# Projection slabs as one 512-column product with the high weights and one of 256 with the low: a bank per quarter of the outputs

## The reference

```python
IN_SPLITS = (GROUP_W, GROUP_W,                              # RG-LRU: gate, input
             GROUP_W, GROUP_W, GROUP_W,                     # short gated convolution: b, c, h
             GLA_HEADS * GLA_DK, GLA_HEADS * GLA_DK, GROUP_W, GROUP_W, GLA_RANK,   # GLA: q, k, v, g, rank 16
             GROUP_W, GROUP_W, GROUP_W)                     # attention: q, k, v
o = o * lax.rsqrt(jnp.mean(o * o, -1, keepdims=True) + RMS_EPS)      # end of GLA
...
return o * jax.nn.silu(g)
...
for e in range(N_EXPERTS):
    h = jax.nn.silu(xt @ w_gate[e]) * (xt @ w_up[e])
    out = out + combine[:, e:e + 1] * (h @ w_down[e])
```

## Time and profile before

| | |
|---|---|
| median of 3 runs | 1715.86 us (1712.81 to 1719.31) |
| profiled execution | 1714.94 us, its span 1713.2 us |
| PE busy | 1553.8 us, 91% of the span |
| DVE busy | 945.7 us, 55% |
| ACT busy | 546.2 us, 32% |
| projections | to about 387 us, and again from about 858 to 1229 us |
| granted TensorE clock, mean | 0.962 of 2.4 GHz |

### The profile page before, as it was taken

How to read it: one execution, slowest core, us unless ns; L and a number is a source line. 1 busy time by engine, 2 the same in 40 slices (tenths; PEclk the granted TensorE clock), 3 DMA queues, 4 the chain that set the end, 5 groups by cost and what they waited for, 6 DMA issues and landing times.

```text
span 1713.2 us, 38421 instructions
## 1 busy us (share of the span) xinstructions
PE 1553.8 (91%) x16224; PEld 1090.1 (64%) x16224; DVE 945.7 (55%) x1548; ACT 546.2 (32%) x694; POOL 50.2 (3%) x36
## 2 busy tenths in 40 slices
PE   8999999998899999966599999999997999996664
PEld 8999999884444555422299999998743555452221
DVE  7657655647455556623466476566374556652235
ACT  4553543323222222201265544533321222221112
POOL 0004000000000000000000050000000000000000
PEclk9999999999999999988899999999999999998887
DMA  8655556659999999999965555567589999999996
GB/s 296 216 169 191 170 177 223 244 212 383 420 420 421 420 420 421 420 421 420 396 201 185 165 194 178 162 240 294 235 347 420 420 421 421 421 420 420 421 421 250
DMA packets 138709, 543.88 MB, mean 317 GB/s; under 512 B 23012, under 2 KB 26312, under 8 KB 88536
## 3 DMA queue, kind: packets, MB, share of 16 engines
q1 hardware_dynamic: 138196, 541.97, 81.0%
q10 hardware_dynamic: 388, 0.04, 0.0%
HBM read 539.88 MB, written 2.10 MB: 316 GB/s over the span
## 4 chain that ended last, share of the span: by engine, by line
PE 68%; SPq 15%; DMA 10%; DVE 4%; issue 1%; DVEq 1%; ACT 1%; ACTq 0%
PE ps L826 23%; PE ps L1102 11%; PE ps L988 10%; SPq L408 10%; PE ps L1120 6%; PE ps L823 5%; DMA room<-in_w_up_dram 5%; DMA room<-in_w_down_dram 4%; SPq L412 4%; PE ps L1044 3%; PE ps L1059 3%; PE ps L1079 1%; PE ps L1052 1%; DVE room L1160 1%; DVE w_lo L1160 1%
## 5 line engine op out<-in xcount | busy, mean ns | idle before, releaser
L1102 PE MATMUL ps<-room 128*32 128x256 f32 x5344 | 336.4, 408 | 91.9 <-DMA room<-in_w_up_dram 91.5
L1160 DVE TENSOR_TENSOR w_lo<-room,w_hi 128x2048 fp32r<-128x2048 f32 (+1 forms) x121 | 276.2, 2292 | 228.9 <-ACT w_hi L535 228.4
L1102 PEld LDWEIGHTS ps<-room 128*32 128x32 f32 x5344 | 193.0, 116 | 244.6 <-DMA room<-in_w_up_dram 87.6
L826 PE MATMUL ps<-hT_hi,w_hi 128*128 128x256 f32 x1152 | 329.7, 286 | 1.1 <-DVE w_lo L1160 0.7
L826 PE MATMUL ps<-hT_lo,w_hi 128*128 128x256 f32 x1152 | 326.0, 283 | 0.0
L826 PE MATMUL ps<-hT_hi,w_lo 128*128 128x256 f32 x1152 | 325.9, 283 | 0.0
L535 ACT ACTIVATE w_hi<-room 128x2048 fp32r<-128x2048 f32 x120 | 228.0, 1911 | 228.4 <-PE ps L826 101.7
L1160 DVE TENSOR_TENSOR h<-h,ps 128x512 f32<-128x512 f32 (+1 forms) x380 | 241.7, 698 | 13.7 <-PE ps L1059 13.6
L1160 DVE TENSOR_TENSOR room<-room,ps 128x128 f32<-128x128 f32 (+2 forms) x53 | 18.5, 353 | 400.1 <-ACT room L742 396.7
L826 PEld LDWEIGHTS ps<-hT_hi,w_hi 128*128 128x128 f32 x1152 | 220.9, 192 | 4.7 <-issue 2.4
L826 PEld LDWEIGHTS ps<-hT_hi,w_lo 128*128 128x128 f32 x1152 | 221.0, 192 | 0.7 <-issue 0.5
(11 more groups left out here) (254 smaller groups left out, 1650.0 us busy)
## 6 DMA issues: line engine op xcount, KB each, us to landing
room<-in_w_down_dram SPq DMA_DIRECT2D x116, 1024.0 KB, 22.0
room<-in_w_gate_dram SPq DMA_DIRECT2D x114, 1024.0 KB, 25.3
room<-in_w_up_dram SPq DMA_DIRECT2D x114, 1024.0 KB, 26.8
room<-in_w_in_dram SPq DMA_DIRECT2D x88, 1024.0 KB, 5.0
room<-in_w_out_dram SPq DMA_DIRECT2D x32, 1024.0 KB, 5.2
spare<-in_w_gate_dram SPq DMA_DIRECT2D x14, 1024.0 KB, 24.8
spare<-in_w_up_dram SPq DMA_DIRECT2D x14, 1024.0 KB, 26.7
spare<-in_w_down_dram SPq DMA_DIRECT2D x12, 1024.0 KB, 17.9
```

What stands on the lines that cost most here:

```text
L826: last = eng.matmul(ps[:, b + o // 2, (o % 2) * T:(o % 2) * T + T], w_[:, o * P:o * P + P], x_[:, kk, :], start=opens and o % 2 == 0, stop ...
L1102: last = eng.matmul(ps[r0:r0 + BLK, 0, 0:2 * P], xe[:, x0:x0 + BLK], unit_gu(u)[:, :, k, c * P:c * P + P], start=(i == 0 and k == 0), stop ...
L1160: return eng.tensor_tensor(o, a, b, op)
```

## The change

Seven slabs (`MERGED`: 1, 3, 4, 5, 7, 8, 9) use w_hi once for both halves of the input. hT_hi and hT_lo become one buffer, `hT_parts`, and the product of the high weights has 512 moving columns, 256 of the high and 256 of the low input, which land side by side in a bank. The low weights then add to its first 256 columns. Each of the four outputs so has a bank of its own (0 to 3), and the sum of its two halves is made later: ACT copies the cross half (`copy_cross`), DVE adds the first half to it (`add_cross`) and counts `bank_free`. Silu and Gelu are then applied in place. Slabs 0, 2, 6 and 10 keep their form and all use banks 0 and 1. At its first quarter a slab waits bank by bank; slabs 1, 3 and 7 begin with outputs 2 and 3.

```diff
+    MERGED = (1, 3, 4, 5, 7, 8, 9)
+    EVACUATED = (0, 2, 5, 6, 7)
...
+                def copy_cross(s, dst, scale=1.0):
+                    for o in range(4):
+                        if o < 3:
+                            eng.wait_ge(o_done.sem, o_done.at(l, 3 * MERGED.index(s) + o + 1))
+                        else:
+                            eng.wait_ge(w_used.sem, w_used.at(l, 4 * s + 4))
+                        eng.activation(dst[:, o * T:o * T + T], ps[:, o, T:2 * T], ACT.Copy, scale=scale
+                                       ).then_inc(cross_copied.sem, 1)
+
+                def in_place(s, dst, func):
+                    eng.wait_ge(bank_free.sem, freed(l, s))
+                    for i in range(2):
+                        eng.activation(dst[:, i * 512:i * 512 + 512], dst[:, i * 512:i * 512 + 512], func
+                                       ).then_inc(z_evac.sem, 1)
...
+                copy_cross(1, r_x)
                 rounds(11, 12)
-                evacuate(1, r_x)
...
-                rounds(18, 20)
+                rounds(18, 19)
                 eng.wait_ge(qk_ready.sem, qk_ready.at(l, 1))
-                evacuate(3, a_qT, scale=float(P) ** -0.5)
+                copy_cross(3, a_qT, scale=float(P) ** -0.5)
+                rounds(19, 20)
...
-                rounds(25, 28)
-                evacuate(5, c_g, ACT.Silu)
+                rounds(25, 27)
+                copy_cross(5, c_g)
+                rounds(27, 28)
+                in_place(5, c_g, ACT.Silu)
...
-                rounds(34, 36)
-                evacuate(7, r_g, ACT.Gelu_apprx_tanh)
+                rounds(34, 35)
+                copy_cross(7, r_g)
+                rounds(35, 36)
+                in_place(7, r_g, ACT.Gelu_apprx_tanh)
...
-                    if first == 0 and s >= 2:
-                        eng.wait_ge(z_evac.sem, z_evac.at(l, 2 * (s - 2) + 2))
...
+                        order = (2, 3, 0, 1) if q == 0 and s in (1, 3, 7) else range(2 if token_major else 4)
+                        for ks, o in itertools.product(parts, order):
...
+                            if q == 0 and s:
+                                bank = o if token_major or joined else o // 2
+                                if s in (1, 3, 7) and bank < 2:
+                                    eng.wait_ge(z_evac.sem, evacuated(l, s - 1, bank + 1))
+                                elif s > 1:
+                                    before_it = s - 2 if s in (3, 7) else s - 1
+                                    eng.wait_ge(bank_free.sem, freed(l, before_it, bank))
...
+                                if joined:
+                                    c = slice(o * P, o * P + P)
+                                    eng.matmul(ps[:, o, :], hi[:, c], hT_parts[:, :, kk, :], start=opens, stop=False)
+                                    last = eng.matmul(ps[:, o, 0:T], lo[:, c], hT_hi[:, kk, :], start=False, stop=ends)
+                                    continue
...
+                            if joined and q == 3 and o < 3:
+                                last.then_inc(o_done.sem, 1)
...
+                def add_cross(s, dst, scale=1.0):
+                    for o in range(4):
+                        eng.wait_ge(cross_copied.sem, cross_copied.at(l, 4 * MERGED.index(s) + o + 1))
+                        sl = dst[:, o * T:o * T + T]
+                        eng.scalar_tensor_tensor(sl, ps[:, o, 0:T], scale, sl, ALU.mult, ALU.add).then_inc(bank_free.sem, 1)
...
                     eng.reciprocal(c_rs[:, 512 * i:512 * i + 512], c_rs[:, 512 * i:512 * i + 512])
                     splits(26 + i, 27 + i)
+                    if i == 0:
+                        add_cross(5, c_g)
...
-                splits(32, 37)
-
-                eng.wait_ge(z_evac.sem, z_evac.at(l, 16))
+                splits(32, 35)
+                add_cross(7, r_g)
+                splits(35, 37)
+
+                eng.wait_ge(z_evac.sem, evacuated(l, 7))
```

More of the change, by code:

```diff
@@ L270, in trunk, with evacuated, freed @@
         hT_rounded, hT_split = signal("hT_rounded", 5), signal("hT_split", 5)
-        z_evac = signal("z_evac", 2 * (N_IN - 1))
+        z_evac = signal("z_evac", 2 * len(EVACUATED))
+        o_done, cross_copied, bank_free = (signal(n, k * len(MERGED)) for n, k in (
+            ("o_done", 3), ("cross_copied", 4), ("bank_free", 4)))
+        def evacuated(l, s, i=2):
+            return z_evac.at(l, 2 * EVACUATED.index(s) + i)
+        def freed(l, s, o=3):
+            return bank_free.at(l, 4 * MERGED.index(s) + o + 1)
         out_first, res_add = signal("out_first", 1), signal("res_add", 2 * N_OUT)
@@ L649, in _ @@
                 last.then_inc(at_ready.sem, 1)
-                rounds(21, 24)
+                rounds(21, 23)
                 eng.wait_ge(u_ready.sem, u_ready.at(l, 1))
-                evacuate(4, a_kT)
+                copy_cross(4, a_kT)
+                rounds(23, 24)
                 eng.wait_ge(om_ready.sem, om_ready.at(l, 1))
@@ L819, in project @@
                                 hi, lo = w_hi[n % 4][:, k, :], w_lo[n % UNITS][:, k, :]
+                                opens, ends = kk == 0, kk == KD - 1
+                                if joined:
[3 more added lines that the diff above has]
+                                    continue
                                 for j, (x_, w_) in enumerate(((hT_hi, hi), (hT_hi, lo), (hT_lo, hi))):
[L821 to L824, removed]
+                                    if token_major:
+                                        last = eng.matmul(ps[:, o, :], x_[:, kk, o * P:o * P + P], w_,
+                                                          start=opens and j == 0, stop=ends and j == 2)
                                     else:
-                                        last = eng.matmul(ps[:, b + o // 2, (o % 2) * T:(o % 2) * T + T],
+                                        last = eng.matmul(ps[:, o // 2, (o % 2) * T:(o % 2) * T + T],
                                                           w_[:, o * P:o * P + P], x_[:, kk, :],
-                                                          start=opens and o % 2 == 0, stop=ends and o % 2 == 1)
+                                                          start=opens and j == 0 and o % 2 == 0,
+                                                          stop=ends and j == 2 and o % 2 == 1)
+                            if joined and q == 3 and o < 3:
+                                last.then_inc(o_done.sem, 1)
                             if between and (q, o) in between:
@@ L1336, in _ @@
                     softplus()
-                splits(18, 21)
+                splits(18, 19)
+                add_cross(3, a_qT, float(P) ** -0.5)
+                splits(19, 21)
                 eng.wait_ge(at_ready.sem, at_ready.at(l, 1))
@@ L1414, in _ @@
                 splits(37, 39)
+                add_cross(8, b_c)
                 rest_mix(1, 8)
@@ L1417, in _ @@
                 rest_mix(2, 0)
-                splits(41, 44)
-                eng.wait_ge(z_evac.sem, z_evac.at(l, 20))
+                splits(41, 43)
+                add_cross(9, b_h)
+                splits(43, 44)
+                eng.drain()
                 eng.wait_ge(att_o.sem, att_o.at(l, 1))
```

27 lines of the change are left out of this document (15 added, 12 removed).

## The result

The changed kernel takes 1775.22 us (median of its undisturbed runs, 1774.34 to 1775.78; one run at 2008 us, and one at 2537 us of a version below, are left out of all that follows). The kernel before took 1716.78 us beside it. The ratio is 1.034, with an interval of [1.0326, 1.0355]: slower, by 58 us. The profiled execution took 1775.78 us, its span 1774.1.

A forecast was written before the change was run, and what follows sets the result against it. PE's chain, 68% of the span, was taken as the bound. To 1714.94 us it added 42.0 (waits less the products' saving, two layers) and 12.0 (half clock): 1768.9, with the median's 0.9 above taken as 1770; range 1745 to 1790.

The forecast's parts named there:

- four waits for banks: PE waits ahead of slabs 2, 6 and 8 and inside slab 7: 3.0, 8.9, 6.0 and 8.7 us a layer.
- the 0.2 us foreseen at slab 9: Behind slab 8, DVE's addition ends at 251.8, PE's slab at 251.5; a wait of 0.2 us was charged.
- Rival 4: Bank handover hidden, decided on DVE behind slab 5; only the product saving is left, 1704 us; chance 0.05.
- three waits of a layer at 2.0 us: Half clock behind each wait of 6.0 us or more (slabs 6, 7, 8): 2.0 us each, 12.0 us in all.
- the wait of 3.0 us: Ahead of slab 2; charged no clock loss, being shorter than the trace's 4.24 us gap; could be 2.0 us twice.
- Rival 1: The waits are there but PE's clock holds in the projections: 1758 us; chance 0.13.
- 347.0 ns: One 512-column plus one 256-column product, against 359.9 ns for three of 256: 5.8 us saved a layer.
- Rivals 2 and 5: The pair of products takes 360 ns, so nothing is saved: 1782 us; chance 0.07 together.
- What lies otherwise in idle time: Removed evacuations, extra copies, in-place Silu and Gelu and additions lie in ACT's and DVE's idle half, costing nothing.
- One to one: What PE gains or loses in the projections moves the expert stage as a whole, in both layers.
- Rival 3: Delay partly absorbed as expert loads fill more slots while PE waits: 1743 us if one layer's 27 us vanished; chance 0.05.

The follow-up runs named there:

- the order with all mends: Changed kernel with the copies, additions and evacuation at slabs 1, 5, 6 and 7 moved ahead of what held them up: 1709.67 us, ratio 0.9966.
- the single mend behind slab 1: Changed kernel with only slab 1's copies moved ahead of the exponentials and its additions ahead of the split of quarter 10: 1768.65 us, ratio 1.0301.
- the fillers: Changed kernel with unused 128-column products ahead of slabs 2 and 6: 20 and 62 of them 1781.94 us, 12 and 38 of them 1769.53 us.
- The two versions with the mends: Changed kernel with all four handovers moved early: with the 512-column product 1709.67 us, with it split again into two of 256 columns 1715.57 us.
- three products, all waits: Changed kernel with its four waits kept, but the 512-column product split again into two of 256 columns: 1784.14 us, ratio 1.04.

## Why the prediction was right, and where its sizes were off

The forecast was 1770 us (1745 to 1790), with the slowdown from four waits for banks. It came out at 1775.2.

**The waits: right, place and size.** Worked out were 3.0, 8.9, 8.7 and 6.0 us a layer. Measured were 3.1, 9.0, 8.8 and 6.2, each released by the step that the prediction named. No wait for an addition showed at slabs 4, 5, 9 or 10; the 0.2 us foreseen at slab 9 are within what these sums can tell. Each of the four was taken away alone, and most of its time came back each time, all of it with the four together (the layers are 34.5 and 35.2 us shorter then). One reading was rounded off (71.32 + 0.37 is 71.7 for the first copy behind slab 1, not 71.6); the split of quarter 10 ends as late, so nothing hangs on it. Rival 4, the hidden handover, was wrong for this order; it is right for the order with all mends, which is why that version gains. It decides where the prediction had put it: the first addition comes early if it doesn't stand behind the split of quarter 25.

**The clock: the mis-sized term.** It stood at 12 us, three waits of a layer at 2.0 us. There were four. Slab 2 lost 2.8 us a layer, slab 6 2.0, slab 7 about 1.3 (9.5 - 8.8 of waiting + 0.6 saved by the pair), and slab 8 about 2.7 (1.4 + 1.3 saved). That is about 9 us a layer, 18 in all. The prediction charged nothing to the wait of 3.0 us, since the earlier trace rows only had a longer gap, and the single mend behind slab 1 and the fillers both showed it to be 2.7 in this kernel. In other versions the same place cost 0 to 2.8, so that term is a range and not a number, and that the first three came out near 2.0 on average is partly luck. The Trainium skill's rule that it weighed (TensorE: Matmul & The Clock Gate, "Why this matters for your kernels": no idle gaps between bursts) had put the 3.0 us waits in danger too. By that rule the sum was 4 us higher; the trace of the kernel after agrees with the rule (2.8 us at 0.50 in each layer), and two waits of 2.6 and 2.9 us in other versions passed without a loss. Rival 1, that the clock holds, is refuted by the stretches at 0.50.

**The pair: right in kind, too hopeful in size.** 347.0 ns was the sum of two rows, and that length is there, but only part of the time; the mean of 350.0 saves 64 x 9.8 ns = 0.63 us a slab, 4.4 us a layer instead of 5.8. The two versions with the mends differ by 3.3 to 3.5 a layer, the rest going into short waits. Rivals 2 and 5 (360 ns) are out. The gap of 2.5 ns that the same page of the Trainium skill gives for an isolated product ("Back-to-back issue gap") isn't what this stream shows either: the columns of the pair alone are 320 ns, so its two products carry 26.7 or 33.3 ns, 13.3 or 16.7 each.

**What lies otherwise in idle time: right.** With all copies and additions in time, four banks cost 0.8 us a layer.

**One to one: right.** The projections of the two layers grew by 32.0 and 32.5 us, the expert stage between them changed by 0.3. Rival 3, the absorbed delay, is out.

From 1768.9 to the profiled 1775.8: + 6 for the clock, + 3 for the pair, - 4 for the shorter stretch behind the last projections, + 2 in remainders under 0.5 us each. No kernel here has an edit in that stretch, and yet it took between 569.0 and 573.4 us in the twelve profiles. Its cause stays open, and that it went the right way here to hide more than half of the clock's excess is luck.

## What to carry to other kernels

When a stage fills more PSUM banks at a time, the copies that free them become urgent. On engines that work in written order, look at what stands between the last product and the first copy, and move it, with the rounding and the addition that the handover needs, ahead of everything that hangs on another engine; here that decided between 58 us lost and 7 us won. Charge each new TensorE wait as long as those here (3.0 to 9.0 us) with its own length and, as an estimate from them, with 1 to 3 us of half clock behind it, and judge a cheaper product only after the handover is hidden.

## What the runs showed of the hardware that wasn't expected

- A pause of 3.0 us was enough for a granted clock of 0.50 afterwards (72 to 78 us), at 2.7 us of lost time, more than the 1.3 to 2.0 us behind the waits of 9 us at slabs 7 and 6 of the same kernel. The loss behind one and the same wait varied from kernel to kernel: slab 6 took 21.8 us at the full clock, and 23.4 to 24.9 behind its wait of 9 us; the first 48 products of slab 2 took 11.1 us at the full clock, and 12.5 to 14.0 behind a wait of 3.05 us. Two waits of 2.63 and 2.64 us in one execution (three products, all waits) cost nothing and 1.6 us.
- A 512-column and a 256-column product in turn take 346.7 or 353.3 ns, constant within an uninterrupted stream, also with the operand's pieces side by side. Three of 256 take 359.8 to 359.9 in all three kernels that have them.
- A filler product of 128 columns in f32 is two instructions on PE, 0.22 to 0.24 us together (24 instructions in 2.84 us, for 12 fillers).
- Four additions of 256 columns with one operand in PSUM took 1.40 us on DVE, not the 1.67 of the earlier trace rows, and four copies out of PSUM on ACT 1.18 us, not four times the 0.37 of the earlier trace rows.
